# Last layer: two pairs of weight blocks in seven products each, and a reciprocal made of Ln and Exp

## The reference

```
h = rms_norm(x, norm_w[1])
xb, g = split(h @ odd_w_in, [2560])                  # 2048 x 5120
xc = sum(xp[:, j:j + T] * conv_w[j] for j in range(4)) + conv_b
r = sigmoid(einsum('btnd,nde->btne', xc in 10 blocks of 256, w_a) + b_a)
i = sigmoid(einsum('btnd,nde->btne', xc in 10 blocks of 256, w_i) + b_i)
log_a = -8 * softplus(-lam) * r
a = exp(log_a)
u = sqrt(max(-expm1(2 * log_a), 0)) * (i * xc)
hr[t] = a[t] * hr[t-1] + u[t]
x = x + (hr * silu(g)) @ odd_w_out                   # 2560 x 2048
out = rms_norm(x, final_norm_w)
```

## Time and profile before

| what | value |
|---|---|
| median of 3 runs | 2723.89 us (2723.53 to 2724.08) |
| the profiled execution, its own time | 2723.69 us |
| its span | 2722.0 us |
| PE busy, share of the span | 2689.2 us, 99% |
| DVE busy | 1506.2 us, 55% |
| ACT busy | 567.9 us, 21% |
| TensorE clock granted, mean | 0.998 |

### The profile page before, as it was taken

The page is one execution under the profiler, slowest core; times in us unless marked ns, Lnnn a source line. Parts: engine busy times, 40 slices in busy tenths (PEclk is TensorE's granted clock), DMA queues, the critical chain, the costliest instruction groups (busy, mean ns, idle before and its releaser), DMA issues.

```text
span 2722.0 us, 50465 instructions
## 1 busy us (share of the span) xinstructions
PE 2689.2 (99%) x19140; PEld 2504.6 (92%) x19140; DVE 1506.2 (55%) x3320; ACT 567.9 (21%) x1344; POOL 281.1 (10%) x473
## 2 busy tenths in 40 slices
PE   8999999999999999999999999999999999999997
PEld 6888889999999999899999999999999999888897
DVE  6666666565565555544444443555545665444555
ACT  3121221110010012333333320112211012222201
POOL 0111010010010000222222210211210000000000
PEclk9999999999999999999999999999999999999999
DMA  6344333444444444333333325433334444444442
GB/s 239 134 144 139 132 131 124 168 155 159 158 162 158 154 156 183 122 125 124 137 124 125 137 94 194 152 128 132 135 137 153 157 170 170 154 154 139 170 155 108
DMA packets 63737, 400.99 MB, mean 147 GB/s; under 512 B 6800, under 2 KB 13472, under 8 KB 17440
## 3 DMA queue, kind: packets, MB, share of 16 engines
q1 hardware_dynamic: 62976, 397.62, 41.0%
q0 software_dynamic: 672, 2.11, 0.5%
HBM read 397.60 MB, written 2.11 MB: 147 GB/s over the span
## 4 chain that ended last, share of the span: by engine, by line
PE 96%; DVE 2%; issue 1%; ACT 1%; DVEq 0%; POOLq 0%; ACTq 0%
PE psum L576 43%; PE psum L522 34%; PE psum L531 6%; PE psum L839 2%; PE psum L1007 1%; PE psum L649 1%; PE psum L748 1%; PE psum L656 1%; PE psum L961 1%; PE psum L672 1%; PE psum L682 1%; PE psum L903 1%; PE psum L959 0%; PE psum L561 0%; DVE h L1491 0%
## 5 line engine op out<-in xcount | busy, mean ns | idle before, releaser
L522 PE MATMUL psum<-h,ring 128*128 128x256 f32 x4256 | 947.1, 380 | 0.9 <-DVE h L1491 0.9
L522 PEld LDWEIGHTS psum<-h,ring 128*128 128x128 f32 x4256 | 797.6, 190 | 117.7 <-issue 14.3
L576 PE MATMUL psum<-mix,ring 128*128 128x128 f32 x3226 | 385.5, 276 | 0.4
L576 PEld LDWEIGHTS psum<-mix,ring 128*128 128x128 f32 x3226 | 372.1, 192 | 2.8 <-DVE near L1567 1.4
L576 PE MATMUL psum<-h,ring 128*128 128x128 f32 x3088 | 366.5, 275 | 0.7 <-DVE near L1567 0.4
L576 PEld LDWEIGHTS psum<-h,ring 128*128 128x128 f32 x3088 | 355.3, 192 | 1.4 <-issue 0.8
L1569 DVE TENSOR_TENSOR near<-psum,near 128x128 f32<-128x128 f32 x95 | 27.7, 292 | 343.6 <-PE psum L576 343.6
L531 PEld LDWEIGHTS psum<-ring,h 128*128 128x128 f32 x1536 | 175.3, 192 | 1.2
L531 PE MATMUL psum<-ring,h 128*128 128x128 f32 x1536 | 175.4, 275 | 0.0
L1062 ACT ACTIVATE w<-psum 128x128 f32<-128x128 f32 x87 | 24.2, 278 | 541.6 <-PE psum L576 541.6
L576 PE MATMUL psum<-ring 128*128 128x128 f32 x1024 | 126.2, 276 | 0.0
(11 more groups left out here) (411 smaller groups left out, 3283.2 us busy)
## 6 DMA issues: line engine op xcount, KB each, us to landing
ring<-w_out SPq DMA_DIRECT2D x80, 1024.0 KB, 5.1
ring<-w_odd SPq DMA_DIRECT2D x64, 1024.0 KB, 5.0
ring<-w_hgrn SPq DMA_DIRECT2D x64, 1024.0 KB, 4.8
ring<-w_even SPq DMA_DIRECT2D x48, 1024.0 KB, 5.0
ring<-w_nsa SPq DMA_DIRECT2D x48, 1024.0 KB, 6.0
ring<-w_rg SPq DMA_DIRECT2D x40, 1024.0 KB, 4.9
ring<-w_cmp_in SPq DMA_DIRECT2D x8, 1024.0 KB, 4.9
ring<-w_rgg SPq DMA_DIRECT2D x10, 512.0 KB, 5.6
```

Of the source, the lines that this page charges most:

```text
L522: mm = pe.matmul(dst[:, 0:T], tile(ph, n, k), h[:, k, :], start=k == 0, stop=k == KT - 1)
L576: mm = pe.matmul(dst, stationary, moving, start=new and j == 0, stop=new and j == kh - 1, skip_group_check=not new)
```

## The change

The turns 1 to 9 of the phase `rg` use `block_products`: `fast_rg` has two pairs, one for `xb` (x) and one for `g` (z), so PE issues 7 + 7 products of 8 matmuls with 128 columns instead of 4 of 16 with 256. The eight gate matmuls stand between the third and the fourth product of the z pair, and their banks are now 6 and 7. A turn has 14 units instead of 5, and its slots come free at units 6, 7, 13, 14 and 11. The first turn stays plain but multiplies all four blocks with `raw_last`, and DVE scales them as it reads them (`from_raw`).

DVE's tail of turn i - 1 is cut in two: `decays(i - 1)` and `outputs(i - 1)` stand inside turn i. The reciprocal 1 / (1 + e) is no DVE instruction any more: DVE adds 1 (`one_plus`), ACT takes Ln and then Exp with scale -1. The weight forms use `wides` (lower half), the activation sums `sums_rg` lie in their upper half.

```
+        rg = Phase(RGB, 14, [Load(n, tiles("w_rg", n), SLOT, (6, 7, 13, 14)[n]) for n in range(4)] +
+                   [Load(7, tiles("w_rgg", 0), 8 * P, 11)])
...
             def rg_block(i, first):                                  # PE
-                product(rg, i, 1, bank[1], h_from=3 * KT if first else None)
-                pe.wait_ge(rgg_used, after(i))
-                product(rg, i, 2, bank[4])
...
                 if first:
+                    wait_load(pe, rg, 0, 0)
                     unscaled(lambda k: tile(rg, 0, k), bank[0][:, 0:T], raw_last, 3 * KT, lambda: norm(2))
+                    plain(1, bank[1], 6)
+                    plain(2, bank[3], 1)
+                    gates()
+                    plain(3, bank[4], 6)
+                    pe.wait_ge(h_ready, after(4 * KT))
                 else:
+                    block_products(fast_rg, i, 0, of_h, sums_rg, 60)
+                    block_products(fast_rg, i, 1, of_h, sums_rg, 60, None, (), ((3, gates),))
...
+                s.wait_ge(rg_gated, after(i + 1))                    # ACT
...
+                st.mark(s.activation(w5[:, :, :], w3[:, :, :], ACT.Ln))
+                st.settle()
+                s.activation(w5[:, :, :], w5[:, :, :], ACT.Exp, scale=-1.0).then_inc(rg_log, 1)
+                s.wait_ge(rg_mixed, after(i))
+                if not first:
+                    s.wait_ge(used, done(rg, i, 12))
+                    s.activation(z_rg[:, 0, 0:P], bank[3][:, 0:P], ACT.Copy).then_inc(first_read, 1)
...
+            def from_raw(pair, dst, first_bank, units):              # DVE
+                for e in range(2):
+                    v.wait_ge(used, done(rg, 0, units[e]))
+                    copied = v.tensor_tensor(dst[:, e, :], bank[first_bank + e][:, 0:T], rstd[:, :], ALU.mult)
+                    copied.then_inc(later_read if e else first_read, 5 if e else 2)
...
+            one_plus(0)
+            three_forms(fast_rg, 1, 0)
+            from_raw(1, z_rg, 3, (8, 14))
+            fourth_form(fast_rg, 1, 0)
...
+            def rg_block(i, last):                                   # DVE, turns 1 to 9
+                first_sum(fast_rg, i, 0)
+                decays(i - 1)
+                constants(i)
+                two_sums(fast_rg, i, 0, x_rg)
+                three_forms(fast_rg, i, 1)
+                fourth_sum(fast_rg, i, 0, x_rg)
+                fifth_sum(fast_rg, i, 0, x_rg)
+                fourth_form(fast_rg, i, 1)
+                convolve(i)
+                first_sum(fast_rg, i, 1)
+                outputs(i - 1)
+                one_plus(i)
+                two_sums(fast_rg, i, 1, z_rg)
...
+                    three_forms(fast_rg, i + 1, 0)                   # or of fast4, in the last turn
+                fourth_sum(fast_rg, i, 1, z_rg)
+                fifth_sum(fast_rg, i, 1, z_rg)
...
+            rg_block(RGB - 1, True)
+            decays(RGB - 1)
+            outputs(RGB - 1)
```

More of the change, by code:

```diff
@@ L305, in pieces @@
                 out.append(([at(e, n * w, (n + 1) * w) for n in range(4)],
[L306 removed]
+                            [s[:, 0:w] for s in f.spare_rest]))
             return out
@@ L990, in rg_block, with gates @@
             def rg_block(i, first):
-                pe.wait_ge(xb_ready, after(2 * i))
+                def gates():
+                    pe.wait_ge(xc_ready, after(2 * i + 2))
+                    wait_load(pe, rg, i, 4)
+                    pe.wait_ge(rg_a, after(i))
+                    for g in range(2):
+                        for e in range(2):
+                            for c in range(2):
+                                mm = pe.matmul(bank[6 + g][:, e * T:(e + 1) * T], at(7, (4 * g + 2 * e + c) * P,
+                                                                                     (4 * g + 2 * e + c + 1) * P),
+                                               w2[:, c, :], start=c == 0, stop=c == 1)
+                    mm.then_inc(rg_gated, 1)
@@ L993, in rg_block, with plain @@
+                def plain(n, dst, units):
+                    wait_load(pe, rg, 0, n)
+                    for k in range(KT):
+                        mm = pe.matmul(dst[:, 0:T], tile(rg, n, k), raw_last[:, k, :], start=k == 0, stop=k == KT - 1)
+                    mm.then_inc(used, units)
                 if first:
-                    wait_load(pe, rg, i, 0)
+                    wait_load(pe, rg, 0, 0)
                     unscaled(lambda k: tile(rg, 0, k), bank[0][:, 0:T], raw_last, 3 * KT, lambda: norm(2))
-                else:
-                    product(rg, i, 0, bank[0])
@@ L1326, in _, with root @@
             norm(3)
-            with s.Fori(0, RGB) as i:
-                for c in range(2):
[L1330 to L1341, removed]
-                s.wait_ge(rg_r, after(i + 1))
+            def root(i):
+                s.wait_ge(rg_v, after(i + 1))
+                s.activation(w6[:, 0, :, :], w3[:, :, :], ACT.Sqrt, scale=0.25).then_inc(rg_s, 1)
@@ L1347, in _ @@
                 ins.then_inc(rg_a, 1)
[L1348 to L1352, removed]
+                s.wait_ge(first_read, after(2 * z_pair + 2))
+                s.wait_ge(later_read, after(5 * z_pair + 5))
+                s.activation(z_gate, z_rg, ACT.Tanh, scale=0.5).then_inc(rgg_tanh, 1)
@@ L1353, in _ @@
+                st.leave(1 if first else RGB - 1)
+            rg_block(0, True)
+            with s.Fori(1, RGB) as i:
+                rg_block(i, False)
+            root(RGB - 1)
             block_reads(fast4, 4, 0, 32, 3)
@@ new lines, in _ @@
+            x_rg = xpad[:, :, 4:T + 4]
+            constants(0)
+            v.sem_inc(forms_made, 4)
+            from_raw(0, x_rg, 0, (1, 7))
+            convolve(0)
+            v.wait_ge(h_ready, after(4 * KT))
+            sums(sums_rg, h[:, 0:8, :], h[:, 8:16, :], 56)
+            one_plus(0)
[16 more added lines that the diff above has]
+                two_sums(fast_rg, i, 1, z_rg)
+                if last:
+                    three_forms(fast4, 0, 0)
+                else:
+                    three_forms(fast_rg, i + 1, 0)
+                fourth_sum(fast_rg, i, 1, z_rg)
+                fifth_sum(fast_rg, i, 1, z_rg)
+                if last:
+                    fourth_form(fast4, 0, 0)
+                else:
+                    fourth_form(fast_rg, i + 1, 0)
```

124 lines of the change are left out of this document (71 added, 53 removed).

## The result

The changed kernel takes 2707.64 us (median of 4 runs, 2706.71 to 2708.14) where the kernel before took 2723.86 beside it: the ratio is 0.994 with an interval of 0.9926 to 0.9955, so 16.2 us or 0.6% faster. The profiled execution took 2706.71 with a span of 2705.0 us, 17.0 under the span of before. The forecast was 2708.4 with a range of 2703 to 2716.5. Of all executions reported here one, of the last experiment, ran at a mean granted clock of 0.947 and took 2744.6 us, and it is left out of every comparison.

The account below looks back on a forecast made before the run. PE's own matmul issue was taken to bound the kernel, DVE and ACT being covered. The terms -23.5 + 1.4 - 0.8 + 4.4 + 2.15 + 1.0 gave -15.35 us from 2723.69, about 2708.4, range 2703 to 2716.5.

Parts of the forecast that it names:

- seven products for eight, 9 turns: Turns 1 to 9 of `rg`: a turn takes 28.47 us against 31.08, saving 23.5 us in nine turns.
- gates wait for the convolution: In each turn PE waits 0.15 us before the gates for DVE's convolution: 1.4 us in all, bounds 0 to 4.5.
- no wait for `h` in turn 0: First turn: raw activations do away with the wait for `h`, saving 0.8 us.
- pause before turn 1: Between turns 0 and 1 PE idles 4.4 us for `from_raw`, which stands behind the three forms; bounds 2.2 to 4.4.
- clock behind it: After the pause before turn 1 the granted clock may fall: 1.0 us put in, between 0 and 2.6.
- behind the last turn: In the output projection's first turn PE waits longer for the last block's `mix`: 2.15 us, at most 3.
- The rival of a late convolution: Convolution's four waits cost 0.3 us each, gates 1.1 us later each turn: +10, 2718 us; chance 0.12.
- The table loads: Rival: two loads between gates and ACT's copy each hold ACT 1.4 us longer: +9, 2717 us; chance 0.04.
- The transfers: Loads for the z pair land 4.8 to 6.4 us after issue, in time for the forms: no cost.

Follow-up runs that it names:

- the last experiment: Changed kernel with the mended seam, plus the fourth form of the output projection's first pair moved behind that pair's first sum: 2699.88 us median.
- mended seam: Changed kernel with turn 1's three forms and fourth form made ahead of the z reads, without waiting for turn 0's end: 2701.06 us.
- filled pause: Changed kernel with nine matmuls of unused result behind turn 0's last plain product: 2705.47 us.
- serial convolution: Changed kernel with the convolution in the old order, one half after the other, each instruction behind the wait for the one before: 2710.65 us.
- two tail runs: Mended seam plus the output projection's first fourth form moved behind the last turn's outputs (2701.08 us), or behind its pair's first sum (2699.88 us).

## Why the prediction was right

By its own terms, against the profiled executions:

| term | forecast us | measured us | from |
|---|---|---|---|
| seven products for eight, 9 turns | -23.5 | -23.5 | turn of 28.47 for 31.08 |
| gates wait for the convolution | +1.4 | 0 | no wait on L2225 |
| no wait for `h` in turn 0 | -0.8 | -0.8 | 21.15 us to the gates for 21.92 |
| pause before turn 1 | +4.4 | +4.3 | 2299.43 to 2303.75; mended seam |
| clock behind it | +1.0 | +1.7 | 3.40 + 1.90 for 2 x 1.79; filled pause |
| behind the last turn | +2.15 | +1.3 | 10.16 for 8.85 |
| sum | -15.35 | -17.0 | spans 2705.0 and 2722.0 |

The terms close, but that the forecast came within 0.8 us of the median is in part luck. The gates and the tail were 2.25 us too dear and the clock 0.7 us too cheap, and the profiled execution (2706.71) was the fastest of four.

**The mechanism of the gain** was that of the forecast: nothing but PE's issue, with every other engine covered. What carried it is the slack, and three runs put a price on it: the convolution had hardly any (0.37 us more cost 0.36 a turn), ACT's copy about 1.9 us (3.8 more cost a wait of 1.9 a turn), and DVE before unit 13 about 1.7 (3.4 more cost a wait of 1.66 a turn, where the prediction had 0.7 of slack and the expectation a wait of 2.0). So the layout of the turn by hand was right in its order and put the events of its second half 0.4 to 0.7 us too late: `outputs` began at 17.7 and not 18.1, `one_plus` ended at 23.0 and not 23.7.

**The gates' term** was too large because I put 0.15 us of waiting behind a convolution that just fitted. The pairs took 0.91 (2.72 for three, 0.9 in the prediction) and the convolution ended where I had it (17.54 us into the turn for 17.6). The whole way from that end to the weight load, with the three register instructions in it, was 0.22 us. That the term is 0 and not some tenths is luck: the serial convolution shows that 0.37 us more would have come through in full. The rival of a late convolution named the right place. Its price of 0.3 us for each wait did not come: the first L2225 starts 0.03 us behind L2219. In the loop the first small sum L1550 starts 0.33 us behind the end of `mix` (2326.57 to 2326.90), and in the last turn, which is written out, 0.03 (2554.17 to 2554.20).

**The seam.** Both the releaser (`from_raw`, not the forms) and the size were right, and moving the two forms ahead took the pause away. The clock's term of 1.0 was a middle between 0 and 2.6, for want of a case to decide it. The clock fell, and filling the pause gave 1.6 of its 1.7 us back at turn 1. The size is not fixed, though. Three experiments left the seam as it is, and the serial convolution's profile shows the same wait of 4.15 us with more behind it:

```profile
2304.23 3.79 PE L583 MATMUL psum<-h,ring 128*128 128x128 f32 x16 [4.15 <-DVE prob L2265]
2307.80 2.67 PE L583 MATMUL psum<-wide_b,wide_a 128*128 128x128 f32 x16
2310.31 1.95 PE L583 MATMUL psum<-wide_a,wide_b 128*128 128x128 f32 x16
```

Two products take 6.08 us there for 3.57, a loss of 2.5. With the reciprocal on DVE it is 3.0, with Ln and Exp twice 1.7. The granted clock fell to 0.50 at 2302.4, 1.8 us before the first product, in the first of these; 0.8 us before it in the second; and 1.1 us behind its start in the third. So the same pause cost 1.7 to 3.0 us, and the changed kernel's profile shows the low end. That this also makes the scatter of 1.4 us between its executions is likely, but not shown.

**The tail** was mis-sized by 0.85 us. I let the last turn's forms begin 24.35 us into the turn, but they began at 23.84 (23.93 in turn 1). The sums ahead of them waited for PE's product and not for DVE:

```profile
2556.52 0.29 DVE L1613 TENSOR_TENSOR near<-psum,near 128x128 f32<-128x128 f32 x1 [0.48 <-PE psum L583]
...
2557.05 1.22 DVE L1572 TENSOR_TENSOR wide_b<-ring 128x1024 f32<-128x1024 f32 x1
```

So the fifth sum ended 0.5 us behind PE's last product and not 1.1, and the fourth form took 1.4 us and not 1.6 until `decays` began. The written-out `outputs` were faster too (2550.85 to 2555.22, 4.4 us for 5.0), but that isn't what moved the forms. The two tail runs show in addition that the wait for `mix` was only where DVE's queue first showed; the bound was all the work ahead of the sum L1606. Moving the form behind that sum brought PE's fourth product forward by 1.45 us.

**The table loads** cost 1.28 us each, with 0.01 us between a load and its activation, so that rival fell. The Trainium skill ("ScalarE: Activation LUTs", What ACT_TABLE_LOAD costs) adds 1380 ns of drain to a load; by that rule, Ln and Exp twice would have cost some 67 us, an estimate from four drains of 1.4 us on top of the 1.9 that PE waited in each of nine turns. The trace disagrees: it has 0.01 us between load and activation, and the run took 17.7 us more.

**The transfers** landed in time in every turn: the half-sized gate load took 6.8 to 7.8 us behind the others, those of `w_rg` 4.7 to 7.5, and no engine waited for a load in the loop.

Of the 17.0 us between the profiled executions nothing is left unexplained; the 16.2 us of the medians differ from it by less than the scatter of 1.4 us between executions. What stays open is which pause takes the clock down and for how long; it fell in each of the five profiles looked at, four with 4.3 us and one with 2.6.

## What to carry to other kernels

When PE is the bound and a scheme moves work from it to DVE, write down one turn with the times at which PE wants each result, and look for the interval between two of PE's events that holds the longest chain; its slack, and not the busy share, decides. Look at the seams (first turn, last turn, change of phase) apart: there a wait that is right inside the loop may protect nothing, and an instruction that merely stands behind it holds the next phase. Where an engine's queue is full up to an instruction that another waits for, reordering in front of that instruction gained nothing here; only what was moved behind it did.

## What was not expected of the hardware

A pause of 2.6 us in front of PE's second product was enough for a granted clock of 0.50 (1.2 GHz) in the work behind it, at a cost of 1.7 us. A pause of 4.3 us cost 1.7 us in two profiles, 2.5 and 3.0 in two others, and the clock fell now in the pause and now up to 1.1 us behind its end. Work of no use in the pause kept it at 1.00.
